# A two-layer attention block behind an RWKV block on one core: another order in its attention steps and in its top-k selection

## What is computed

```python
def dsa_attention(...):                     # layer A, 8 heads, blocks of 128 queries
    q, k, v, qi, ki, wi = jnp.split(h @ w_in, A_SPLITS, axis=-1)
    ...
    s = jnp.einsum('bqhd,bsd->bqhs', qib, ki) * IDX_DIM ** -0.5      # 8 index heads
    score = jnp.einsum('bqh,bqhs->bqs', wib, jax.nn.relu(s))
    score = jnp.where(vis[None], score, NEG_INF)
    _, idx = lax.top_k(score, k_top)                                 # 128 keys of each query
    ...
    p = jax.nn.softmax(logits, axis=-1); o = p @ v[idx]
    return out @ w_o

def diff_attention(...):                    # layer B, 8 heads, two maps each, all keys
    a = attn_map(q1b, k1) - lam * attn_map(q2b, k2)
    ...
```

## Time and profile before

| | us |
|---|---|
| median of 3 runs | 2372.32 |
| lowest, highest | 2370.37, 2376.07 |
| the profiled execution | 2370.89 |
| its span in the trace | 2369.6 |
| layer A, from the first `a_in` product to the first product of `residual` | 964 to 1243 |
| layer B's attention | 1740 to 1950 |

### The profile page before, as it was taken

How to read it: one execution, slowest core, us unless ns; L and a number is a source line. 1 busy time by engine, 2 the same in 40 slices (tenths; PEclk the granted TensorE clock), 3 DMA queues, 4 the chain that set the end, 5 groups by cost and what they waited for, 6 DMA issues and landing times.

```text
span 2369.6 us, 44580 instructions
## 1 busy us (share of the span) xinstructions
PE 2222.9 (94%) x19538; PEld 1949.6 (82%) x19538; DVE 1458.7 (62%) x2296; ACT 943.5 (40%) x1600; POOL 460.2 (19%) x261
## 2 busy tenths in 40 slices
PE   4898999999988999987899999999999999999999
PEld 1677777777766777877679999999988889999987
DVE  3687888888866444398336667633355556677722
ACT  1324334334332434423554444322456654444411
POOL 0444333333310344433221000000000011000000
PEclk7899999999998999988899999999999999999999
DMA  6531011111124334310013333323311013222231
GB/s 231 135 109 54 11 42 42 42 42 42 42 87 153 99 94 125 104 45 23 10 31 108 91 92 95 90 88 99 104 48 40 19 37 116 90 90 90 85 107 67
DMA packets 57986, 184.74 MB, mean 78 GB/s; under 512 B 6944, under 2 KB 6944, under 8 KB 57792
## 3 DMA queue, kind: packets, MB, share of 16 engines
q1 hardware_dynamic: 57792, 181.89, 24.6%
HBM read 174.99 MB, written 6.88 MB: 77 GB/s over the span
## 4 chain that ended last, share of the span: by engine, by line
PE 70%; DVE 20%; ACT 6%; issue 2%; DMA 1%; POOL 0%; SPq 0%; DVEq 0%; ACTq 0%
PE PS L534 55%; DVE ca L1867 5%; PE PS L664 4%; PE PS L1018 2%; PE PS L1145 1%; PE PS L1113 1%; PE PS L859 1%; DVE Swk L2266 1%; DVE mx L2262 1%; DVE kx L1935 1%; DVE Bf L1941 1%; DVE Ssc L2242 1%; ACT Lb L1193 1%; DMA xt<-in_xT 1%; ACT tB L1193 1%
## 5 line engine op out<-in xcount | busy, mean ns | idle before, releaser
L2553 POOL TENSOR_TENSOR wlo<-raw,whi 128x1024 fp32r<-128x1024 f32 (+1 forms) x138 | 306.3, 2221 | 936.7 <-ACT whi L1193 936.7
L534 PE MATMUL PS<-nhi,whi 128*128 128x264 f32 x2064 | 441.6, 295 | 9.3 <-DVE nlo L2108 8.5
L534 PE MATMUL PS<-nlo,whi 128*128 128x264 f32 x2064 | 424.1, 288 | 0.0
L534 PE MATMUL PS<-nhi,wlo 128*128 128x264 f32 x2064 | 421.5, 286 | 0.0
L1193 ACT ACTIVATE whi<-raw 128x1024 fp32r<-128x1024 f32 (+2 forms) x306 | 303.5, 993 | 229.8 <-PE PS L534 202.0
L534 PEld LDWEIGHTS PS<-nhi,whi 128*128 128x128 f32 x2064 | 325.2, 191 | 19.6 <-DVE qB L2150 5.6
L534 PEld LDWEIGHTS PS<-nlo,whi 128*128 128x128 f32 x2064 | 325.7, 191 | 0.0
L534 PEld LDWEIGHTS PS<-nhi,wlo 128*128 128x128 f32 x2064 | 324.8, 191 | 0.0
L1779 DVE TENSOR_TENSOR wlo<-raw,whi 128x1024 fp32r<-128x1024 f32 (+1 forms) x168 | 201.1, 1197 | 171.8 <-ACT whi L1193 171.6
L534 PE MATMUL PS<-hhi,whi 128*128 128x512 f32 x648 | 263.8, 407 | 6.7 <-DVE hlo L1846 6.6
L534 PE MATMUL PS<-hhi,wlo 128*128 128x512 f32 x648 | 258.1, 398 | 2.9 <-POOL wlo L2553 2.9
(11 more groups left out here) (351 smaller groups left out, 3541.0 us busy)
## 6 DMA issues: line engine op xcount, KB each, us to landing
raw<-in_wall SPq DMA_DIRECT2D x282, 512.0 KB, 3.6
raw<-in_wall SPq DMA_DIRECT2D x32, 256.0 KB, 2.7
raw<-in_wall SPq DMA_DIRECT2D x16, 384.0 KB, 3.1
TZ<-g_rows SPq DMA_DIRECT2D x2, 2112.0 KB, 8.8
g_rows<-gsb SPq DMA_DIRECT2D x8, 328.0 KB
xt<-in_xT SPq DMA_DIRECT2D x1, 2048.0 KB, 13.4
o_rows<-os SPq DMA_DIRECT2D x8, 256.0 KB, 2.2
keep<-o_rows SPq DMA_DIRECT2D x8, 256.0 KB, 4.4
```

The lines of the kernel that those rows point to most:

```text
L534: q = e.matmul(out, cuts[a][:, k * P:(k + 1) * P], (hi_, lo_)[b][:, kr, lo:lo + w], start=start and k == 0 and a == b == 0, stop=stop and ...
L2553: e.tensor_tensor(wlo[slot[i]][:, w], raw[i % NRAW][:, w], whi[slot[i]][:, w].bitcast(F32), ALU.subtract).then_inc(*up("lo_pool", i))
```

## The change

1. `SELECT` is another string. The s steps come at g = 19, 27, 35, 41, 51, ... 90 (before 21, 29, 37, 42, 45, ... 71). On DVE the scores now hang on a letter of their own, "d", one to three g behind each s. The r steps begin at g = 44, right behind block 3's scores, and end at g = 126. Of the "a", 24 stand before g = 136, 50 at it, 55 after it; the first a comes at g = 95 (before 87).
2. `rel` has four buffers in place of two.
3. The norm of an `a_in` unit is put off to contraction step 5 of the next unit.
4. In an iteration of layer A's attention DVE takes the maximum and negative of step n first and then the inverse of step n - 1 (before: the inverse first). ACT does exponential n and then scales step n - 1 (before: scaling first, and a third of an iteration earlier). Layer B's loop is turned in the same way, and its second scaling on DVE moves from iteration n + 1 to n + 2.
5. In layer A ACT copies the transposed tiles of steps 0 to 4 and DVE those of all others (before: ACT the even steps, DVE the odd). Layer B keeps the old division.

The program has the same matmuls, transfers and POOL instructions as before.

```diff
--- before.py
+++ after.py
@@ -31,10 +31,11 @@
 SLOT = 1024
 
 
+
 FIRST = 5
-SELECT = ("g" * 16 + 3 * "gggggsggg" + "ggsgggsggsg" + 2 * "gsgrgrgsgrgrgsgr" + "gsgrgsgrgsgrgsgr" + "grgrgrgrgggg"
-          + "grgrgrgrgrgrgraagr" + 4 * "grgragrgrgrgrgraagr" + "gar" + 3 * "aagag" + 9 * "aaga" + 8 * "aaa"
-          + 3 * ("aagag" "aagag" "aagag" "aaga" "aaga") + 4 * "aagga")
+SELECT = ("g" * 16 + 3 * "gggsggdggg" + "gsggdgrgrgrgrgr" + "grgrgrsgrgrdggg" + "sgrgrdgrsgrdgggg" + "sgrgrdgrgrgggg"
+          + "sgrgrdsgrgrdsgrdggg" + "sgrgrdsgrgrdsgrdggg" + "sgrgrdsgrgrdgrgrgraag" + 4 * "grgragrgrgrgraagg"
+          + "gag" + 3 * "aagag" + 16 * "aaa" + 3 * ("aagag" "aagag" "aagag" "aaga" "aaga") + 4 * "aagga")
 BESIDE = "aagggaagg" "aaaagggg" "aagaaggg" "aaaagg" "aaaag"
 AFTER = "aaggaagg" "aaaagg" "aaagg" "agg" "aagg" "aagg"
@@ -385,7 +386,7 @@
         kiT = blockmem("kiT", T)
         wiT = blockmem("wiT", T)
         qiT = grid(blockmem("qiT", 4 * T), 4)
-        rel = grid(blockmem("rel", 2 * T), 2)
+        rel = grid(blockmem("rel", 4 * T), 4)
         wtok = grid(blockmem("wtok", 4 * 8), 4)
         mask = [blockmem(f"mask{i}", WIDTH[i]) for i in range(4)]
         kT = grid(blockmem("kT", 2 * T), 2)
@@ -496,9 +497,13 @@
         def nothing():
             return iter(())
 
+        def by_act(name, n):
+
+            return n < FIRST if name == "a" else n % 2 == 0
+
         def turned_by(name, n):
 
-            return (name + ("_PT" if n % 2 else "_PT_act"), n)
+            return (name + ("_PT_act" if by_act(name, n) else "_PT"), n)
 
         def rest_at(w):
@@ -897,7 +902,7 @@
             def steps_of(what, b, hi_, lo_, rhs=None):
 
                 for k, _ in enumerate(product(what, hi_, lo_, halves(T, b), rhs)):
-                    if k == (1 if what in ("a_out", "b_out") else 3):
+                    if k == (1 if what in ("a_out", "b_out") else 5 if what == "a_in" else 3):
                         flush()
                     yield
...
@@ -1535,9 +1540,9 @@
                         for n in range(2):
                             h = 2 * t + n
                             on.wait_ge(*at("index", i, h))
-                            if h >= 2 or i < 3:
-                                on.wait_ge(*at("score", i if h >= 2 else i + 1, (h - 2) % 8))
-                            act(sv(rel[:, n, 0:w], w), psv(w, first[n]), ACT.Relu, scale=0.125).then_inc(*up("rel", i, h))
+                            if h >= 4 or i < 3:
+                                on.wait_ge(*at("score", i if h >= 4 else i + 1, (h - 4) % 8))
+                            act(sv(rel[:, h % 4, 0:w], w), psv(w, first[n]), ACT.Relu, scale=0.125).then_inc(*up("rel", i, h))
                         yield
 
             def attend_a():
...
@@ -1568,9 +1573,6 @@
                     act(pt[0:rem, whole, 0:nq], PS[0:rem, b, c0:c0 + nq], ACT.Copy).then_inc(*up("a_PT_act", n))
 
                 for n in range(N + 4):
-                    if 1 <= n <= N:
-                        on.wait_ge(*at("a_inv", n - 1))
-                        act(row(n - 1), row(n - 1), ACT.Copy, scale=cell(n - 1, 2)).then_inc(*up("a_weights", n - 1))
                     yield
                     if 3 <= n <= N + 2:
                         h, i = steps[n - 3]
@@ -1580,6 +1582,9 @@
                     if n < N:
                         on.wait_ge(*at("a_neg", n))
                         act(row(n), row(n), ACT.Exp, bias=cell(n, 1), accum_out=cell(n, 2)).then_inc(*up("a_exp", n))
+                    if 1 <= n <= N:
+                        on.wait_ge(*at("a_inv", n - 1))
+                        act(row(n - 1), row(n - 1), ACT.Copy, scale=cell(n - 1, 2)).then_inc(*up("a_weights", n - 1))
                     yield
                     if 2 <= n <= N + 1:
                         turn(n - 2)
...
@@ -1718,14 +1723,14 @@
                         act(sqb[:, 0:T], oTb[:, h % 3, :], ACT.Square).then_inc(*up("ob_sq", h))
 
                 for n in range(N + 6):
+                    yield
+                    if 3 <= n <= N + 2:
+                        apply(n - 3)
+                    yield
+                    if n < N:
+                        scores(n)
                     if 1 <= n <= N:
                         weights(n - 1)
-                    yield
-                    if 3 <= n <= N + 2:
-                        apply(n - 3)
-                    yield
-                    if n < N:
-                        scores(n)
                     yield
                     if 2 <= n <= N + 1:
                         turn(n - 2)
...
@@ -2239,7 +2244,7 @@
                             e.tensor_scalar(Ssc[i][:, :], rel[:, 0, 0:w], wc, None, ALU.mult).then_inc(*up("score", i, h))
                         else:
                             on.wait_ge(*at("score", i, h - 1))
-                            e.scalar_tensor_tensor(Ssc[i][:, :], rel[:, h % 2, 0:w], wc, Ssc[i][:, :], ALU.mult,
+                            e.scalar_tensor_tensor(Ssc[i][:, :], rel[:, h % 4, 0:w], wc, Ssc[i][:, :], ALU.mult,
                                                    ALU.add).then_inc(*up("score", i, h))
                         if h % 2:
                             yield
...
@@ -2343,7 +2348,7 @@
                                         ALU.subtract).then_inc(*up("oa", h))
                     yield
 
-            run(SELECT, a=attend_a(), s=select(), r=rounds(), g=made_a())
+            run(SELECT, a=attend_a(), s=nothing(), d=select(), r=rounds(), g=made_a())
 
             def residual(name, gname, gj, n_units, last=False, after=None):
                 n, c0 = (S, 16) if last else (T, 0)
...
@@ -2503,10 +2508,10 @@
 
                 for n in range(N + 6):
                     wide = n < N and steps[n][1] == 3
-                    if 1 <= n <= N:
-                        inverse(n - 1)
                     if n < N:
                         scores(n, 0)
+                    if 2 <= n <= N + 1:
+                        weights(n - 2)
                     yield
                     if n < N and not wide:
                         scores(n, 1)
@@ -2514,7 +2519,7 @@
                     if wide:
                         scores(n, 1)
                     if 1 <= n <= N:
-                        weights(n - 1)
+                        inverse(n - 1)
                     yield
                     if 2 <= n <= N + 1:
                         turn(n - 2)
...
```

More of the change, by code:

```diff
@@ L1032, in attend_a @@
                 free2[4], free2[6] = [*four[4], *four[5]], [*four[6], *four[7]]
-            run(SELECT, a=attend_a(), s=select(), r=nothing(), g=made_a())
+            run(SELECT, a=attend_a(), s=select(), d=nothing(), r=nothing(), g=made_a())
             def residual(what, name, hi_, lo_, rhs, n_units=1, last=False, first=0):
@@ L1492, in made_a @@
             def made_a():
-                yield from steps_of(8, 3)
+                yield from steps_of(8, 5)
                 on.wait_ge(*at("ki_raw"))
@@ L1559, in turn @@
                     whole, rem, pt = w // P, w % P, PTa[n % 2]
-                    if n % 2:
+                    if not by_act("a", n):
                         return
@@ L1696, in turn @@
                     whole, rem, pt = w // P, w % P, PTb[n % 2]
-                    if n % 2:
+                    if not by_act("b", n):
                         return
@@ L1728, in attend @@
                         scores(n)
+                    if 1 <= n <= N:
+                        weights(n - 1)
                     yield
@@ L2317, in turn @@
                     whole, rem, pt = w // P, w % P, PTa[n % 2]
-                    if n % 2 == 0:
+                    if by_act("a", n):
                         return
@@ L2493, in turn @@
                     pt = PTb[n % 2]
-                    if n % 2 == 0:
+                    if by_act("b", n):
                         return
@@ L2696, in attend_a @@
                     yield
-            run(SELECT, a=attend_a(), s=nothing(), r=rounds(), g=made_a())
+            run(SELECT, a=attend_a(), s=nothing(), d=nothing(), r=rounds(), g=made_a())
             while units[count.next][0] != "b_kv":
```

## The result

| | time, us | span of the profiled execution |
|---|---|---|
| before | 2370.3, median of 6 (2369.3 to 2376.1) | 2369.6 |
| after | 2382.2, median of 6 (2381.2 to 2384.3) | 2379.9 |
| after / before | 1.0047, 95% interval 1.0034 to 1.0060 | |

What follows compares the result with a forecast made beforehand. The prediction took PE as the bound, except DVE during layer A's selection. Its terms put `residual` at 1232.9 instead of 1242.7 us, 9.8 us less, with layer B unchanged: 2361.1 profiled, 2362.5 median, range 2352 to 2377.

Steps and rivals of the forecast that it cites:

- The start of the rounds: Layer A's selection: the first round on DVE begins at 998.8 us instead of 1009.3, 10.5 us sooner.
- The last mask: End of layer A's selection on DVE: at 1113.5 us instead of 1119.0, with -10 and +10 as ends.
- The two unknowns: In the selection: DVE's idle time, and DVE instructions stretched beside POOL's casts; 2 us of loss taken for both together.
- To g = 136: Layer A, from the last mask to g = 136: 16.3 us, so PE arrives at 1129.8 instead of 1159.2.
- The bare stretch: Layer A's attention alone, before `a_out`: 16.7 iterations at 2.65 us, 44.2 us; `a_out` begins at 1174.0 instead of 1185.2.
- third rival: Half clock holds for layer A's whole bare stretch, 3.5 us per iteration: 2376.8 us, 2380.3 with a late mask; chance 0.14.
- The tail: Layer A's attention beside `a_out`: 58.9 us instead of 58.0, including 1.0 less PE idle time; `residual` begins at 1232.9.
- Parts 4 and 5 in layer A: Layer A's attention: 0.1 us less per bare iteration and 1.0 less PE idle time in the tail; added wait costed at nothing.
- Layer B: Layer B's attention: nothing gained or lost, within 2 us of 210; 15 us if the second scaling's cover were gone.
- The second one: Rival: the selection's gain is eaten, last mask at 1117, bare iterations stay at 2.89 us: 2370.0 us; chance 0.26.
- The slower one: The third rival again: half clock throughout layer A's bare stretch, 14.3 us more than forecast; chance 0.14.
- The sum: Whole program: 2370.9 - 9.8 = 2361.1 us for the profiled execution, 2362.5 for the median.

Runs made afterwards that it cites:

- e12: The e4 kernel with ACT copying the transposed tiles of steps 0 to 4 and all even steps of layer A: 2359.0 us, ratio 0.9958 to the kernel before.
- e11: The e4 kernel with layer A's copies divided as before the change and two buffers of `rel` instead of four: 2358.3 us, ratio 0.9947 to the kernel before.
- e4: The changed kernel with layer B's attention loop and layer A's attention order put back as before: 2354.7 us, ratio 0.9942 to the kernel before.

## Why the prediction was wrong, point by point

- **The start of the rounds**: right. 10.5 us sooner were forecast, 11.7 measured.
- **The last mask**: right in direction and under-sized, 10.1 for 5.5 (end of DVE's last instruction on `Swk`). I had said that I would be wrong if DVE had over 10 us idle there, and it had 15.0 (110 us from 997 to 1107, 95.0 busy). The two unknowns went opposite ways: DVE waited more, 8.0 us of it for POOL's masks (3.0 before), but its instructions were shorter. The last one on `Swk` took 0.37 us, where it took 2.41. Stretched instructions were not moved elsewhere, as I had assumed; they became fewer. That they belong to POOL's work beside them, which I had only supposed, the traces do show (last section). My reading that PE waits here because DVE takes products out between two rounds was loose: PE's two largest waits from 1000 to 1118 us were 10.3 us for ACT's squares and 6.6 for DVE's normed `qall`.
- **To g = 136**: 16.3 us were forecast from the last instruction on `Swk`, 17.9 measured. I had miscounted: at the last r 12 of the "a" are passed now and 15 were before, not 14 and 17. The same sum with the right counts gives 17.4.
- **The bare stretch**: nearly right. 44.2 us were forecast, and from 1124.5 to 1170.7 it took 46.2. A head at half clock took 12.15 us (1145.08 to 1157.23), and one with part of it at full clock 11.17:

```profile
1145.08 2.37 PE L1023 MATMUL PS<-PT,Vk 128*128 128x128 f32 x8 [0.67 <-DVE PT L2331]
...
1157.23 2.37 PE L1023 MATMUL PS<-PT,Vk 128*128 128x128 f32 x8 [0.67 <-DVE PT L2331]
...
1168.40 2.37 PE L1023 MATMUL PS<-PT,Vk 128*128 128x128 f32 x8 [0.67 <-DVE PT L2331]
```

  The second of these heads had a mean clock of .65 and the head of before with its 11.01 us one of .66, so the 0.1 us per iteration that I took off for parts 4 and 5 did not come: 11.17 is 0.04 more per iteration. The clock of the stretch, .61 in the mean, was between my forecast's .67 and the third rival's .5. The third rival's price per iteration (3.5 us) did not occur: 12.15 / 4 = 3.04 in the slower of these two heads.
- **The tail**: mis-sized, and the largest miss in layer A. 58.9 forecast, 64.4 measured (1170.7 to 1235.1). I had taken 1.0 us off for waits; in fact PE's idle time went from 4.4 to 6.7 us (64.00 - 57.32), and from 1171 to 1175 it still ran at a clock of .67.
- **Parts 4 and 5 in layer A**: wrong sign. A credit of 2.7 us stood against a cost of 8 to 10 by the ratios. The sentence that failed is "I cost it at nothing, since the scores come first in PE's iteration". That reasoned over PE's order and left out what is queued behind the new wait on DVE and ACT. The runs show 2 to 3 us at equal low clock, 5 to 7 at equal high clock, and the high clock less often; most of what the profiles show of it arises before g = 136, where I had looked for no effect at all. Why the clock differs stays open.
- **Layer B**: the step that turned the sign is "nothing lost either", the cover of DVE's second scaling. "An iteration is 210 / 40 = 5.25 us ... so it is done some 3 us ahead" takes a mean where the order is uneven. The string `BESIDE` gives the widest step five g and the narrowest a single one, and in three of its five kinds of step the four a stand together: PE goes from the scores over a small product straight to the transposes. I knew the chain and even priced it (15 us if the cover were gone), then left 2 us of that in the range. 17.9 was measured.
- **The rivals**: none of the three happened as told. The second one's last clause, that the new order doesn't do what it says, did come true in layer A, but its late mask did not. The slower one put the price in the clock of the bare stretch. It should have been the uncovered scaling in layer B, whose price stood in my own text. That this price, 15 us, is near the 17.9 measured is partly luck: it was layer A's wait per iteration times 40, and in layer B twenty waits of 0.7 us in the mean came to 13.8, with the clock and slower instructions on top.
- **The sum**: 2370.9 - 9.8 = 2361.1 against 2381.24. With layer A at 5.4 in place of 9.8 and layer B at +17.9 it would have been 2383.4; the 2.2 us over are the earlier start of the changed kernel's profile (967.6 and 965.4).

## What to carry to other kernels

Whether a queued instruction is covered has to be read off the order at the step with the least work between, not from a mean iteration: write down for each kind of step what the waiting engine does between giving and wanting. When an uncovered case was priced and then dropped, the price belongs in the range as long as the order hasn't been walked through. And a change of several parts should be measured in halves: here the string of letters with the later norm gives 14 us, and the two reorderings beside it took back more than that.

## What the runs showed of the hardware

- The stretch with attention alone has no fixed granted clock. From 1120 to 1175 us its mean was .61 in one kernel's profile (e12) and .88 in that of another that differed by little (e11), and executions of one and the same kernel (e4) spread over 19 us, from 2345 to 2364, in step with the mean clock of the span, .976 to .965. The kernel before, whose bare stretch is about half as long, spread over 11 us in 20 executions (2366.7 to 2377.3).
- A wait of PE can cost more than its own length: busy for 1.08 of 2 us at full clock, then 4 us at .62 and .53 without a pause, 1.7 us lost. This followed at two places in layer B, among twenty waits, and makes 3.4 of its 17.9 us.
- Some instructions of DVE are stretched to the end of an instruction that POOL has begun ahead of them. The last one on `Swk` took 2.41 us before, from 1116.57, beside this one of POOL:

```profile
1116.46 2.35 POOL L2553 TENSOR_TENSOR wlo<-raw,whi 128x1024 fp32r<-128x1024 f32 x1 [4.49 <-ACT whi L1193]
```

  In the changed kernel, where POOL stood idle from 1103.7 to 1106.66, it took 0.37:

```profile
1106.21 0.37 DVE L2289 SCALAR_TENSOR_TENSOR Swk<-Ssc,cnt,Swk 128x144 f32<-128x144 f32 x1
```

  It is so throughout the two traces. Of the 64 instructions that add up or mask with two tensors into `Ssc` and `Swk` (`L2242`, `L2284` before, `L2247`, `L2289` after), nine are stretched. Each of them begins while POOL works and ends 0.2 to 0.4 us behind POOL's instruction. The other 55 have their own time (0.36 to 0.77 us): 45 have no instruction of POOL beside them, nine began up to 0.6 us ahead of POOL's, and one began 0.2 us before POOL's end. MAX8 and MATCH_REPLACE8 kept their own time in all 64 cases with POOL at work for over half of it. For this reason the 144-key product into `Ssc` took 0.63 us before and 0.42 after in the mean, and of the 10.1 us by which DVE ends the selection sooner, 2.0 are that its last instruction no longer meets POOL.
